# Identity products in front of eight of TensorE's waits in a three-layer transformer kernel

## The reference

```python
y_b = ssd_mixer(z, xbc, dt_raw, ...) @ w_o_ssd
mix = (jax.nn.sigmoid(g_a) * y_a + jax.nn.sigmoid(g_b) * y_b) @ w_out
x = x + gate_m * rmsnorm(mix, post_norm_mix)
h2 = rmsnorm(x, pre_norm_ffn) * (1.0 + scale_f) + shift_f
```

## Time and profile before

| | before |
|---|---|
| time, median of 3 runs | 2677.68 us (2677.65 to 2678.42) |
| the profiled execution's own time | 2689.04 us |
| its span, first to last instruction | 2685.8 us |
| TensorE busy | 2569.7 us, 96% |
| VectorE, ScalarE, GpSimd busy | 57%, 39%, 37% |
| mean granted TensorE clock | 0.980 |

### The profile page before, as it was taken

The page is one execution under the profiler, slowest core; times in us unless marked ns, Lnnn a source line. Parts: engine busy times, 40 slices in busy tenths (PEclk is TensorE's granted clock), DMA queues, the critical chain, the costliest instruction groups (busy, mean ns, idle before and its releaser), DMA issues.

```text
span 2685.8 us, 35971 instructions
## 1 busy us (share of the span) xinstructions
PE 2569.7 (96%) x14072; PEld 2022.1 (75%) x14072; DVE 1526.0 (57%) x1965; ACT 1043.4 (39%) x1609; POOL 992.5 (37%) x262
## 2 busy tenths in 40 slices
PE   8999889999999889999989999999999998899998
PEld 7777847888877578888867777786668776688886
DVE  6636655543438746442366689973555774544244
ACT  5434444322223543222233355533553553432222
POOL 1336723444443124444433433341004552244443
PEclk9999989999999999999999999999999998899999
DMA  5224512232223002322233333334334331222222
GB/s 182 84 91 172 188 37 94 96 106 96 94 94 101 32 32 97 105 96 94 94 105 118 113 130 126 118 133 143 102 111 145 126 124 55 77 94 94 94 97 91
DMA packets 72389, 280.57 MB, mean 104 GB/s; under 512 B 9891, under 2 KB 27645, under 8 KB 45123
## 3 DMA queue, kind: packets, MB, share of 16 engines
q1 hardware_dynamic: 59875, 259.72, 28.5%
q10 hardware_dynamic: 12384, 19.03, 2.0%
HBM read 259.25 MB, written 19.40 MB: 104 GB/s over the span
## 4 chain that ended last, share of the span: by engine, by line
PE 52%; issue 35%; POOL 8%; DVE 4%; ACT 1%; DMA 0%; POOLq 0%; DVEq 0%; ACTq 0%; SPq 0%
PE banks L585 9%; PE banks L586 9%; PE banks L587 9%; POOL w_lo L3362 8%; PE banks L2738 2%; PE banks L1044 2%; PE banks L1045 2%; PE banks L1046 2%; PE banks L2746 2%; PE banks L1948 1%; PE banks L2847 1%; PE banks L2849 1%; PE banks L2848 1%; PE banks L2760 1%; PE banks L2493 1%
## 5 line engine op out<-in xcount | busy, mean ns | idle before, releaser
L3362 POOL TENSOR_TENSOR w_lo<-raw,w_hi 128x2048 fp32r<-128x2048 f32 x168 | 775.5, 4616 | 1343.7 <-ACT w_hi L564 1294.0
L585 PE MATMUL banks<-hn_hi,w_hi 128*128 128x512 f32 x1880 | 740.1, 394 | 24.4 <-DVE hn_lo L2261 6.6
L586 PE MATMUL banks<-hn_lo,w_hi 128*128 128x512 f32 x1880 | 735.7, 391 | 0.0
L587 PE MATMUL banks<-hn_hi,w_lo 128*128 128x512 f32 x1880 | 735.4, 391 | 0.0
L564 ACT ACTIVATE w_hi<-raw 128x2048 fp32r<-128x2048 f32 x180 | 345.0, 1917 | 608.7 <-PE banks L587 479.7
L585 PEld LDWEIGHTS banks<-hn_hi,w_hi 128*128 128x128 f32 x1880 | 355.3, 189 | 120.2 <-issue 29.0
L587 PEld LDWEIGHTS banks<-hn_hi,w_lo 128*128 128x128 f32 x1880 | 355.2, 189 | 74.7
L586 PEld LDWEIGHTS banks<-hn_lo,w_hi 128*128 128x128 f32 x1880 | 355.6, 189 | 72.5
L1000 DVE TENSOR_TENSOR hid_lo<-prod,hid_hi 128x512 f32 x62 | 282.0, 4548 | 117.6 <-ACT hid_hi L964 117.6
L997 DVE TENSOR_TENSOR prod<-sg,banks 128x512 f32<-128x512 f32 x62 | 42.6, 688 | 240.5 <-PE banks L587 240.5
L585 PE MATMUL banks<-hid_hi,w_hi 128*128 128x512 f32 x416 | 163.1, 392 | 3.3 <-POOL w_lo L3362 3.3
(11 more groups left out here) (578 smaller groups left out, 4080.3 us busy)
## 6 DMA issues: line engine op xcount, KB each, us to landing
raw<-in_W SPq DMA_DIRECT2D x202, 1024.0 KB, 4.8
oh_early<-codes SPq DMA_DIRECT2D x88, 128.0 KB, 3.0
extra<-in_W SPq DMA_DIRECT2D x8, 1024.0 KB, 4.9
spill<-cs ACTq DMA_DIRECT2D x32, 256.0 KB, 2.3
spill<-mem_q ACTq DMA_DIRECT2D x32, 256.0 KB, 2.7
oh_late<-codes SPq DMA_DIRECT2D x40, 128.0 KB, 2.8
grp<-spill SPq DMA_DIRECT2D x8, 512.0 KB, 4.5
grp<-spill SPq DMA_DIRECT2D x16, 256.0 KB, 4.9
```

Of the source, the lines that this page charges most:

```text
L585: pe.matmul(out, wh, xh(k), start=(k == 0), stop=False)
L586: pe.matmul(out, wh, xl(k), start=False, stop=False)
L587: mm = pe.matmul(out, wl, xh(k), start=False, stop=(k == nkt - 1))
L3362: pool.tensor_tensor(w_lo[:, u % 2, :], raw[:, u % 2, :], w_hi[:, u % 2, :].bitcast(F32), ALU.subtract).then_inc(S("w_lo"), 1)
```

## The change

A new helper opens the bank of a key and issues n bf16 products of the identity with itself into it, 128x512 each, whose sums the first real product in the bank overwrites. It is called at eight places with 150 products in all: 11 before the sums of `pe_onorm`, 10 before `wout0`, 30 before `qlat`, 17 at the head of `pe_small_late`, 16 before tile 32 of the mixer, 18 before `wout2`, 36 before `pe_h2` and 12 before the third feed-forward. At `wout0` the wait for `mix_lo` moves behind the wait for the value tiles and the new products; in `pe_small_late` the wait for `keys_scaled` moves behind its new products. No other engine's program changes.

```diff
+        def keep_busy(pe, key, n):
+            open_bank(pe, key)
+            for i in range(n):
+                pe.matmul(bank(key)[:, :], identb[:, :], identb[:, None, :].broadcast_to([P, NC, P]), start=True, stop=True)
...
         def pe_onorm(pe):
-            open_bank(pe, ("onorm",))
+            keep_busy(pe, ("onorm",), 11)
...
         def pe_small_late(pe):
+            key = ("kid",)
+            keep_busy(pe, key, 17)
             pe.wait_ge(S("keys_scaled"), 2)
-            key = ("kid",)
-            open_bank(pe, key)
...
             open_bank(pe, key)
+            if n == 32:
+                keep_busy(pe, key, 16)
             for k in range(nkt):
...
-            pe.wait_ge(S("mix_lo"), HG)
             for j in range(2):
                 taken(pe, ("value", 0, j))
+            keep_busy(pe, ("unit", U["wout0", 0], 0), 10)
+            pe.wait_ge(S("mix_lo"), HG)
             pe_linear(pe, "wout0")
...
             pe_both_squares(pe)
+            keep_busy(pe, ("unit", U["qlat", 0], 0), 30)
             pe_linear(pe, "qlat", ready=ada_ready(pe, 0))
...
+            keep_busy(pe, ("tok", "wout2", 0, 0), 18)
             pe.wait_ge(S("blend_lo"), KT)
             token_unit(pe, "wout2", 0, blended, KT)
...
+            keep_busy(pe, ("h2", 0), 36)
             for j in range(3):
                 pe_h2(pe, j)
+            keep_busy(pe, ("unit", U["gu20", 0], 0), 12)
```

## The result

The changed kernel takes 2685.96 us (median of 8 runs, 2679.92 to 2688.74), the kernel before on the same chip 2678.35 (8 runs, 2670.93 to 2682.76). The ratio is 1.0023, with a 95% interval from 1.0012 to 1.0034: slower by 6.2 us, between 3.2 and 9.1. (The two medians by themselves differ by 7.6 us; the interval belongs to the ratio, so I go by that.) The forecast was slower by 2.2 us. The absolute 2679.9 us can't be compared directly, as the kernel before itself moved from 2677.68 to 2678.35. The profiled execution has a span of 2682.9 us and a time of 2685.09.

A forecast was written before the change was run, and what follows sets the result against it. TensorE, busy 96% of the span, was taken as the bound. Terms 3.1 - 2.1 + 0.7 - 3.7 - 2.7 + 2.5 + 0 gave 2.2 us slower, 2677.68 to 2679.9 us; own range 2677.5 to 2682, wide range 2675 to 2684.8.

The forecast's parts named there:

- 1 norm sums: 11 products before the norm sums fit their 2.87 us wait; the sums then run at full clock: gain 3.1 us.
- 2 wait and `wout0`: 10 products before `wout0` stand behind the value tiles' wait, where bank 0 frees late: loss 2.1 us, between 1.9 and 4.1.
- 3 wait and `qlat`: 30 products before `qlat` just fit the 6.6 us wait; VectorE's input limits the unit: gain 0.7 us, no more.
- 4 `pe_small_late`: 17 products at the head of `pe_small_late` stand where TensorE has no idle time: loss 3.7 us, between 3 and 3.9.
- 5 tile 32 to `wout2`: 16 products before mixer tile 32, which starts without a wait; small later slack absorbs some: loss 2.7 us, between 2.5 and 3.5.
- 6 `wout2`: 18 products before `wout2` lie in a 4.16 us wait; its half-clock start goes to full clock: gain 2.5 us.
- 7, 8 `pe_h2`, feed-forward: 36 and 12 products fit their waits, but VectorE and ScalarE set the pace: nothing, from +0.5 to -1.8 us.
- Identity products: Rival, all eight places: identity products don't hold the clock, so the gains at 1, 3, 6 vanish; 2692.4 us, chance 0.09.
- run over: Rival: clock holds, but late or half-clock blocks cost their bounds, chiefly at `wout0` and `wout2`; 2682 to 2684.4 us, chance 0.15.
- All eight in waits: Rival: all eight blocks lie in waits, so losses 2, 4 and 5 are 0; 2671.4 us, chance 0.05.
- The memory attention: Rival: the memory attention warms up, with 3 to 5 us less at half clock; 2675 to 2677 us, chance 0.13.

## Why the prediction was right or wrong

The sign and most of the reasons held, the size did not. A loss of 6.2 us lies above the forecast's own range, which ended at +4.3 (2682 less 2677.68), within the wide one, which ended at +7.1, and in the part above 2683.0, which had a chance of 0.20. The rivals meant for that part are not what happened. The stages from trace to trace, each between the same two products in every trace (a few bounds lie up to three products beside the stage's own, so the differences count, not the lengths); before as the mean of three traces, after as the mean of two:

| step | forecast | before | after | measured |
|---|---|---|---|---|
| 1 norm sums | -3.1 | 7.4 (8.3, 7.0, 7.0) | 5.3 | -2.1 |
| 2 wait and `wout0` | +2.1 | 16.3 (15.5, 16.8, 16.7) | 17.3 (17.4, 17.1) | +1.0 |
| 3 wait and `qlat` | -0.7 | 21.5 | 21.5 | 0 |
| 4 `pe_small_late` | +3.7 | 0.32 | 4.00 | +3.7 |
| 5 tile 32 to `wout2` | +2.7 | 41.5 (41.6, 41.2, 41.8) | 44.1 | +2.6 |
| 6 `wout2` | -2.5 | 11.4 (11.6, 10.7, 11.9) | 9.2 | -2.2 |
| 7, 8 `pe_h2`, feed-forward | 0 | 29.7 | 29.7 | 0 |
| sum | +2.2 | | | +3.0 |

**The losses (4, 5, and the place of 2)** were right. Three blocks stand where TensorE has no wait, and each product costs its 0.217 us: 17 of them 3.7 us, by the earlier trace rows and the idle time that wasn't there. Tile 32's products move what follows by 3.3 us, and some 0.7 come back before `wout2`: 0.2 in the small wait before the sum, the rest because VectorE's reciprocal now waits for ScalarE's root and no longer for the DMA:

```profile
2209.90 3.35 DVE L3212 RECIPROCAL rs<-rs 128x512 f32<-128x512 f32 x1 [5.64 <-ACT rs L3241]
```

That is the forecast's mechanism, but its size was read from one trace: the reciprocal starts 2.38, 1.92 and 2.53 us after the sum's start in the three traces of before, and 1.85 in both of the changed kernel. In the second trace there was no DMA's lead to take. The doubled blocks show the same price again, and the run with the three dense blocks alone has all of the loss. In step 2 the block took 3.64 us, forecast 3.75, and starts only after L1616, as said.

**The terms that were mis-sized** are all of one kind: the half clock that a filled wait avoids. Step 1 put 3.1 us on the half clock of the sums, and step 2 counted seven real products at half clock in the kernel before, which its block spares (7 x 0.20 = 1.4 us); in the other two traces of before they are some 14 and 12. Both came from one trace, and the length of a half-clock stretch differs between executions: norm sums 8.3, 7.0 and 7.0 us. The first trace had it long in the norm sums and short in `wout0`; against that trace alone step 2 lost 2.0 us, as forecast. So as a mean step 1 gained 2.1 instead of 3.1, step 2 lost 1.0 instead of 2.1, and the two errors cancel in the sum, which is luck.

**Step 3** failed in its mechanism. I took the last block's `hn_lo` as the limit, 0.7 us ahead of TensorE. But VectorE sets the pace at the block before it too, and makes the last two blocks' input back to back, so TensorE's end is that block's start plus two blocks of work. In the timelines of TensorE and VectorE in the changed kernel:

```profile
1388.70 0.50 PE L590 MATMUL banks<-hn_hi,w_hi 128*128 128x512 f32 x1
...
1387.96 1.47 DVE L2266 TENSOR_TENSOR hn_lo<-tmp,hn_hi 128x512 fp32r<-128x512 f32 x2
```

From there it is dense, and the 48 products took 13.50 us where they had taken 13.58. The gain was 0.1, not 0.7, and as a mean over the traces nothing. Nor had half of the blocks been at half clock, as the prediction says: the first 12 of the 48 products were (1385.96 to 1391.22), so that TensorE had caught up with VectorE before the end.

**Steps 7 and 8** held: the transposes take 1.50 us instead of 2.79, but from the first of them to the unit's first product it is 5.89 us (2301.35 to 2307.24) where it was 5.88: TensorE waits for VectorE's L1209 instead. The run without these two blocks lost nothing.

**The rivals.** Identity products do hold the clock, so 2692.4 us fell. The blocks that lie in waits didn't run over. All eight in waits was wrong for the kernel as it stands, as the earlier trace rows said. The memory attention took 45.0 us before and after: it didn't warm up. In two other kernels with the first block it took 43.5; why is not known.

**What stays open** is part of the size. The two comparisons say +6.2 and +5.9 us, the eight places +3.0, all behind the recurrence +4.4. Of the 1.4 us between the last two, 0.9 lie ahead of the mixer and 0.4 between `wout0` and `qlat`, both in half-clock stretches. The one ahead of the mixer may be more than chance. Every trace has a wait of 1.65 us there, 538 us behind `pe_small_late`'s first own product. In the changed kernel:

```profile
1998.86 1.14 PE L2765 MATMUL banks<-ident,pr 128*128 128x128 f32 x8 [1.65 <-ACT pts L2818]
```

Behind it the clock fell in three of the four traces of kernels with the dense blocks (the changed kernel once of twice, the dense blocks alone, the doubled ones), at a cost of 2.8 us each, and in none of the other nine. If the dense blocks bring it about, they cost more than their products; no run tests it, and by what path they would is open. The comparisons of equal kernels strayed by +2.7 us; taken off, some 3.4 would be left, near the sum. Whether that offset also applied to the first comparison wasn't measured. The interval, 3.2 to 9.1 us, holds +4.4 and just misses +3.0.

## What to carry to other kernels

A product put into a wait is free only if its bank is open before the wait begins and the next instruction behind it is what waits; look at the idle time in the row of the instruction right behind the place, because the longest wait of a stage may lie one unit or seven tiles away. Fill a wait only where TensorE sets the pace of what follows: where VectorE does, the faster clock turns into a wait. And read the size of such a gain from several traces, since half-clock stretches at one place last longer in one execution than in another.

## What the runs showed of the hardware

- The granted clock stayed at full after waits filled with bf16 products of the identity, and with float32 transposes of the identity (norm sums 5.36 us both ways, against 7.03 to 8.33). What streams through the array doesn't need to be of use.
- The idle stretch alone doesn't decide: full clock after 3.32 us idle in one place, half after 2.98 us in another of the same execution, and after 1.38 us in one kernel but not in the others. Behind one wait of 1.65 us that all 13 traces have, the clock fell in three of them.
- Executions of one program differ by 12.5 us in their first 350 us (335.22, 339.54 and 347.72 us to the norm sums), more than all eight blocks cost. The mean granted clock over this stretch was 0.97 in the slowest of the three and 0.99 in the fastest. That is some 21 us at half clock (0.03 x 2 x 347.7) against 7, and would make about half of the difference, where the rounding of the clock allows 4 us more or less. What makes the rest is not known.
